# One kernel, its operand tiles moved: pairs of tiles at start addresses of their own

## The reference, cut to what matters

```
proj = rmsnorm(x) @ w_in                       # 1024 x 2048: pool channels, q, k, v
mk, mv = rmsnorm(mem) @ w_ck, rmsnorm(mem) @ w_cv
x = x + concat(pool_mix(u), moba_attend(q, k, v)) @ w_out
x = x + (softmax((rmsnorm(x) @ w_cq) mk^T / 16) mv) @ w_co
x = x + square(relu(rmsnorm(x) @ w_up)) @ w_down   # 1024 x 4096, 4096 x 1024
y = rmsnorm(x)
```

## Time and profile before

| | |
|---|---|
| median of 3 runs | 419.35 us |
| the profiled execution | 421.09 us |
| its span (first to last instruction) | 419.1 us |
| PE (matmuls) busy | 412.7 us, 98% |
| PEld (weight loads, beside the matmuls) | 386.7 us, 92% |
| VectorE (DVE) | 253.1 us, 60% |
| ScalarE (ACT) | 227.0 us, 54% |
| DMA | 96.60 MB, 230 GB/s |

### The profile page before, as it was taken

One profiled execution on the slowest core, in us unless ns is written; L12 is line 12 of the kernel. 1 busy time (PEld: TensorE's weight loads), 2 busy tenths in 40 slices (PEclk: granted clock), 3 DMA queues, 4 the chain that ended last, 5 costly groups with the idle time before them and its releaser, 6 DMA issues.

```text
span 419.1 us, 8425 instructions
## 1 busy us (share of the span) xinstructions
PE 412.7 (98%) x3372; PEld 386.7 (92%) x3372; DVE 253.1 (60%) x400; ACT 227.0 (54%) x392; POOL 30.9 (7%) x41
## 2 busy tenths in 40 slices
PE   9999999999999999999999999999999999999995
PEld 9998989986879998948899999999999999999995
DVE  4799989666355784633259777666667534454302
ACT  5876958725454664424267666566565433453313
POOL 1003026000000220000022000000000000010011
PEclk9999999999999999999999999999999999999999
DMA  8999858965988966989527646555565655545002
GB/s 288 384 386 359 283 194 251 349 253 191 404 295 317 386 218 226 370 309 335 218 102 248 205 141 199 185 187 163 184 200 196 196 172 192 183 158 185 2 2 103
DMA packets 37257, 96.60 MB, mean 230 GB/s; under 512 B 4186, under 2 KB 13274, under 8 KB 37082
## 3 DMA queue, kind: packets, MB, share of 16 engines
q1 hardware_dynamic: 35106, 92.24, 63.3%
q10 hardware_dynamic: 2112, 3.82, 2.5%
HBM read 91.73 MB, written 4.54 MB: 230 GB/s over the span
## 4 chain that ended last, share of the span: by engine, by line
PE 89%; DMA 5%; DVE 2%; SPq 1%; issue 1%; ACT 0%; DVEq 0%
PE psum L1104 75%; PE psum L826 4%; DMA raw<-in_w_in 2%; PE psum L1046 2%; PE psum L941 2%; DMA stage<-in_mem_v 2%; PE psum L954 1%; DMA pages<-in_page_table 1%; PE psum L838 1%; PE psum L878 1%; SPq L772 1%; PE psum L887 1%; PE psum L925 1%; PE psum L947 0%; DVE rstd L1586 0%
## 5 line engine op out<-in xcount | busy, mean ns | idle before, releaser
L1392 DVE TENSOR_TENSOR w_lo<-raw,w_hi 128x1024 fp32r<-128x1024 f32 x67 | 82.4, 1239 | 62.2 <-ACT w_hi L1124 62.0
L1124 ACT ACTIVATE w_hi<-raw 128x1024 fp32r<-128x1024 f32 (+1 forms) x73 | 74.0, 1021 | 60.7 <-PE psum L1104 45.4
L1104 PE MATMUL psum<-mix_hi,w_hi 128*128 128x264 f32 (+1 forms) x288 | 82.8, 287 | 0.0
L1104 PE MATMUL psum<-mix_lo,w_hi 128*128 128x264 f32 (+1 forms) x288 | 81.5, 283 | 0.0
L1104 PE MATMUL psum<-mix_hi,w_lo 128*128 128x264 f32 (+1 forms) x288 | 81.5, 283 | 0.0
L1104 PE MATMUL psum<-act_hi,w_hi 128*128 128x264 f32 x232 | 66.3, 286 | 0.0
L1104 PE MATMUL psum<-act_lo,w_hi 128*128 128x264 f32 x232 | 65.6, 283 | 0.0
L1104 PE MATMUL psum<-act_hi,w_lo 128*128 128x264 f32 x232 | 65.4, 282 | 0.0
L1104 PEld LDWEIGHTS psum<-mix_hi,w_hi 128*128 128x128 f32 x288 | 54.3, 188 | 0.9 <-issue 0.8
L1104 PEld LDWEIGHTS psum<-mix_lo,w_hi 128*128 128x128 f32 x288 | 54.3, 189 | 0.1
L1104 PEld LDWEIGHTS psum<-mix_hi,w_lo 128*128 128x128 f32 x288 | 54.3, 189 | 0.0
(11 more groups left out here) (208 smaller groups left out, 813.7 us busy)
## 6 DMA issues: line engine op xcount, KB each, us to landing
raw<-in_w_down SPq DMA_DIRECT2D x20, 512.0 KB, 3.3
raw<-in_w_up SPq DMA_DIRECT2D x18, 512.0 KB, 4.3
raw_more<-in_w_up SPq DMA_DIRECT2D x14, 512.0 KB, 3.7
stage<-in_mem_v SPq DMA_DIRECT2D x12, 512.0 KB, 6.5
raw_more<-in_w_down SPq DMA_DIRECT2D x12, 512.0 KB, 4.2
stage<-in_cache_v SPq DMA_DIRECT2D x16, 256.0 KB, 6.2
keysT<-in_cache_k SPq DMA_DIRECT2D x16, 256.0 KB, 5.0
keysT<-in_mem_k SPq DMA_DIRECT2D x8, 512.0 KB, 6.5
```

Of the source, the lines that this page charges most:

```text
L1104: mm = pe.matmul(out, a, b, start=first and m == 0, stop=end_ and m == 2)
L1124: return nc.scalar.activation(out, in_, ACT.Copy, scale=scale)
L1392: V.tensor_tensor(lo_of(c), raw_of(c), hi_of(c).bitcast(F32), ALU.subtract).then_inc(w_lo_ready, 1)
```

## The change

The parts of mix and hid are no longer one array with a fixed step. A function lays each tile at a residue of its own, from a list; the next free place with that residue is taken. Two tiles that follow each other (those of one chunk) share a residue. The high and the low part of a pair can have different ones.

```diff
+LINE = 64
+W_AT = 32
+MIX_HI, MIX_LO = [224, 224, 192, 0], [192, 32, 224, 32]
+HID_HI, HID_LO = [0, 32, 64, 96, 128, 160, 192, 224, 224, 224, 224, 224, 224, 240, 208, 16], [0, 32, 64, 96, 128, 160, 192, 224, 0, 32, 64, 128, 160, 240, 208, 16]
+MIX_AT = [r for part in (MIX_HI, MIX_LO) for r in part for _ in range(2)]
+HID_AT = [r for part in (HID_HI, HID_LO) for r in part for _ in range(2)]
...
-        sb("before_mix", [P, 40])
-        mix_hi = sb("mix_hi", [P, KT, PITCH], F32R)[:, :, 0:T]
-        mix_lo = sb("mix_lo", [P, KT, PITCH], F32R)[:, :, 0:T]
+        def tiles(name, columns, residues):
+
+            at, place = columns, []
+            for r in residues:
+                at += (W_AT + r // 4 - at) % LINE
+                place.append(at - columns)
+                at += T
+            whole = sb(name, [P, place[-1] + T], F32R)
+            return [whole[:, x:x + T] for x in place]
+
+        mix = tiles("mix", W_AT, MIX_AT)
+        mix_hi, mix_lo = mix[:KT], mix[KT:]
...
-        sb("before_act", [P, 48])
+        sb("before_act", [P, 8])
         act_hi = sb("act_hi", [P, KT, PITCH], F32R, early)[:, :, 0:T]
+        sb("between_parts", [P, 32], F32, early)
         act_lo = sb("act_lo", [P, KT, PITCH], F32R, early)[:, :, 0:T]
...
-        sb("beside_operands", [P, 1664])
+        sb("beside_operands", [P, 1696])
         raw_more = sb("raw_more", [P, MORE_RAW, CK, CN])
-        sb("before_more", [P, 8])
+        sb("before_more", [P, 40])
         w_hi_more = sb("w_hi_more", [P, MORE_SPLIT, CK, CN], F32R)
         w_lo_more = sb("w_lo_more", [P, MORE_SPLIT, CK, CN], F32R)
-        sb("before_hid", [P, 16])
-        hid_hi = sb("hid_hi", [P, FT, PITCH], F32R)[:, :, 0:T]
-        hid_lo = sb("hid_lo", [P, FT, PITCH], F32R)[:, :, 0:T]
+        hid_tiles = tiles("hid_tiles", 32, HID_AT)
+        hid_hi, hid_lo = hid_tiles[:FT], hid_tiles[FT:]
...
-                            passes = ((wh, mov_hi[:, k + kk, 0:N]), (wh, mov_lo[:, k + kk, 0:N]), (wl, mov_hi[:, k + kk, 0:N]))
+                            passes = ((wh, mov_hi[k + kk][:, 0:N]), (wh, mov_lo[k + kk][:, 0:N]), (wl, mov_hi[k + kk][:, 0:N]))
```

More of the change, by code:

```diff
@@ L1043, in last_by_tile @@
                             wh, wl = hi[:, kk, x * P:(x + 1) * P], lo[:, kk, x * P:(x + 1) * P]
-                            passes = ((wh, hid_hi[:, k + kk, :]), (wh, hid_lo[:, k + kk, :]), (wl, hid_hi[:, k + kk, :]))
+                            passes = ((wh, hid_hi[k + kk]), (wh, hid_lo[k + kk]), (wl, hid_hi[k + kk]))
                             for m, (a, b) in enumerate(passes):
@@ L1082, in _ @@
                 if w in ("in", "out", "co"):
-                    mov_hi, mov_lo = act_hi, act_lo
+                    mov_hi, mov_lo = ([t[:, i, :] for i in range(KT)] for t in (act_hi, act_lo))
                 elif w == "down":
@@ L1095, in _ @@
                             out = psum[:, bank, :]
-                            th, tl = mov_hi[:, k + kk, x * P:(x + 1) * P], mov_lo[:, k + kk, x * P:(x + 1) * P]
+                            th, tl = mov_hi[k + kk][:, x * P:(x + 1) * P], mov_lo[k + kk][:, x * P:(x + 1) * P]
                             passes = ((th, hi[:, kk, :]), (tl, hi[:, kk, :]), (th, lo[:, kk, :]))
@@ L1181, in take_out @@
                         wait_gemm_out(act, g, x)
-                        copy(mix_hi[:, k, :], xT[:, k, :], gains[:, GAIN[w], k:k + 1]).then_inc(stream_hi, 1)
+                        copy(mix_hi[k], xT[:, k, :], gains[:, GAIN[w], k:k + 1]).then_inc(stream_hi, 1)
                         square("c" if w == "out" else "f", k, xT[:, k, :], T)
@@ L1190, in take_out @@
                         act.wait_ge(square_ready, j + 1)
-                        copy(hid_hi[:, j, :], hid[:, 1, j % 2, :]).then_inc(hid_hi_ready, 1)
+                        copy(hid_hi[j], hid[:, 1, j % 2, :]).then_inc(hid_hi_ready, 1)
                     elif w == "down":
@@ L1239, in run @@
                     square("m", k, src, MEM)
-                    copy(mix_hi[:, k, 0:MEM], src, gains[:, GAIN["m"], k:k + 1]).then_inc(stream_hi, 1)
+                    copy(mix_hi[k][:, 0:MEM], src, gains[:, GAIN["m"], k:k + 1]).then_inc(stream_hi, 1)
                     return
@@ L1399, in low_of_square @@
                 dve.wait_ge(hid_hi_ready, j + 1)
-                V.tensor_tensor(hid_lo[:, j, :], hid[:, 1, j % 2, :], hid_hi[:, j, :].bitcast(F32), ALU.subtract).then_inc(hid_lo_ready, 1)
+                V.tensor_tensor(hid_lo[j], hid[:, 1, j % 2, :], hid_hi[j].bitcast(F32), ALU.subtract).then_inc(hid_lo_ready, 1)
             def make_qblock(src, table, first, rows):
@@ L1439, in take_out @@
                             dve.wait_ge(stream_hi, STREAM[w] + low + 1)
-                            less(mix_lo[:, low, :], xT[:, low, :], gains[:, GAIN[w], low:low + 1], mix_hi[:, low, :]).then_inc(stream_lo, 1)
+                            less(mix_lo[low], xT[:, low, :], gains[:, GAIN[w], low:low + 1], mix_hi[low]).then_inc(stream_lo, 1)
                     elif w == "cq":
@@ L1543, in run @@
                     dve.wait_ge(stream_hi, STREAM["m"] + k + 1)
-                    less(mix_lo[:, k, 0:MEM], memory(k), gains[:, GAIN["m"], k:k + 1], mix_hi[:, k, 0:MEM]).then_inc(stream_lo, 1)
+                    less(mix_lo[k][:, 0:MEM], memory(k), gains[:, GAIN["m"], k:k + 1], mix_hi[k][:, 0:MEM]).then_inc(stream_lo, 1)
                     return
```

## The result

The changed kernel took 421.19 us (median of 20 runs, 420.29 to 424.32), the kernel before 419.52 us (20 runs, 418.83 to 420.73). The ratio is 1.0038, 95% interval 1.0026 to 1.0050: 1.1 to 2.1 us slower, where 1.4 us faster was forecast, in a range from 416.8 to 420.8 us.

What follows compares the result with a forecast made beforehand. The prediction took the pace of PE's matmuls as the bound (TensorE busy 98%). Its terms, -1.24 - 0.28 + 0.28 - 0.12 = -1.36 us, took the 419.35 us median to 418.0 us; range 416.8 to 420.8 us.

Steps and rivals of the forecast that it cites:

- the three known points: Matmul paces before the change by residue to the weights: 224 gives 120.0 ns, 64 gives 120.97, 160 gives 121.66.
- the five terms: The forecast's changes in time by stage and tile, summing to -1.36 us.
- straight lines on the circle of 256 between the three known points: Weight matmuls at unmeasured residues: pace interpolated modulo 256 bytes, for example 0 at 120.32 ns, 128 at 121.43.
- the mean of its three passes, hi twice and lo once: Pace of a chunk with unlike high and low residues: averaged from its parts' paces, hi counted twice, lo once.
- Term 3: out, co and w_in's chunks, act_lo moved from 224 to 96: 0.40 ns a matmul, +0.28 us, ends 0 and +1.2.
- Term 1: cq and up, 960 matmuls on mix's four pairs: mean 120.37 ns against 121.66, -1.24 us, ends -3.2 and +1.6.
- Term 2: down, 768 matmuls on hid's sixteen pairs: 120.61 ns against 120.97, -0.28 us, ends -0.8 and +0.8.
- Terms 4 and 5: ck -0.12 us and cv 0 on mix's new places; the attention's moved tiles 0, ends +-0.2 us.
- Rival C: Weight matmuls of mix, act and down: unlike high and low residues break a rhythm; +2.5 us, 421.9 us; chance 0.19.
- turning point of 121.9 ns: Average cost of an unlike pair above which mix and act together lose what down wins, deciding the sign.
- The rule that spoke against the change: TensorE's weight load and moving operand have separate read ports, so no residue would matter and the time would stay.

Runs made afterwards that it cites:

- e5: Changed kernel with act and mix at residue 224, hid's sixteen pairs in down equal at 0, 16, ... 240; one run, 417.58 us.
- e6: Changed kernel with act and mix at 224, hid's high parts all at 0, low parts at 0, 16, ... 240; one run, 418.73 us.
- e1: Changed kernel with act_lo put back from residue 96 to 224, mix and hid keeping their new pairs; 419.81 us, ratio to the kernel before 0.9996.
- e2: Changed kernel with mix back at 160 and hid at 64, so only act_lo at 96 differs from before; 421.06 us, ratio 1.0031.
- e4: As e3, but mix_lo alone at residue 96; 419.37 us, ratio to the kernel before 0.9984.
- e8: Changed kernel with mix at (128, 128), hid at (0, 0) and act at (192, 224); one run, 421.65 us (before 418.92).
- e3: Changed kernel with act, mix and hid all at residue 224, high and low alike; 417.76 us, ratio to the kernel before 0.9951.
- e11: Changed kernel with act at (96, 224), hid at (32, 0) and mix at (96, 96); one run, 425.85 us (before 420.29).
- e9: As e3, with 64 bytes put ahead of everything, weights included, so only absolute addresses move; one run, 417.57 us.

## Why the prediction was wrong

**What held.** PE's pace is the bound; nothing else of the change cost time (ACT, DVE and PE's waits as forecast); the residue to the weights is a cause, and the three known points, 224, 64 and 160, repeated themselves in the chunks of down (120.2, 120.9, 121.8 ns).

**The step that failed is the one before the five terms: "straight lines on the circle of 256 between the three known points", and for a chunk "the mean of its three passes, hi twice and lo once".** Both halves are wrong, as e5 and e6 show. The sum missed by 3.0 us: 1.2 in act, 0.9 in cq and up, 0.7 in down, 0.2 in ck and cv. Its terms:

- Term 3, act: forecast +0.40 ns, +0.28 us. Measured +2.2 ns, +1.50 us (in 0.68, out 0.43, co 0.39). That is as much as the whole measured loss, though with this term alone put right the sum would still have said -0.1 us. Its upper end, +1.2 us, does not follow from its own numbers either: 123.3 ns over the 384 and half of the 312 matmuls is 1.8 us, and the 1.50 lies within that. e1 takes the loss away, e2 makes it alone, e4 gives it to mix: the pair (224, 96) has 122.2 ns, with equal pairs of its parts at 120.0 and 121.5.
- Term 1, cq and up: forecast -1.29 ns, -1.24 us. Measured -0.34 us. (224, 192) was to have 120.28 and has 122.0, (224, 32) 120.21 and 121.5; (192, 224), forecast at 120.55, is at 120.6, which is luck: its chunks settled to 120.0 and lost the rest on the way in, and e8 held it at 120.8. (0, 32), forecast at 120.43, could have 120.0 and had 121.5 because its chunk ended before the stream had settled.
- Term 2, down: forecast -0.28 us, measured +0.43. The five pairs with 224 high were the dear ones, 121.5 to 122.4, and 128 had 123.5.
- Terms 4 and 5: ck and cv together +0.06 us for -0.12. ck was slower by 1.0 ns, not faster: the points of 264 columns do not hold for its 256, as e3 shows. The attention's plain f32 matmuls kept their lengths (3.65 and 1.73 us in both chains).

**Rival C**, that unlike parts break a rhythm, was the nearest, and its price for act (1.6 ns for each matmul) was in the right place and too small. That its total of 421.9 us lies near is in part luck: its largest term was +1.6 us in mix, which measured -0.34. It made every unlike pair dear, but (0, 32), held long enough, has the best pace there is. Its turning point of 121.9 ns is also worked out wrongly: 960 matmuls of mix and 384 of act at one pace lose the 0.28 us that down was to win at 121.4 ns.

**The rule that spoke against the change.** The distances in e3, e5 and e11 are 120.0, 123.5 and 126.7 ns for the same instruction with no wait, and e9 shows that relative places count. The Trainium skill (SBUF — State Buffer, "Who interferes with whom") has PE with two independent read ports and says that PE waits on no one. If nothing held PE's reads up, no residue would matter, and here it does, by up to 6.7 ns; the measurement decides. That the two reads of PE hold each other up is the nearest reading and not shown: what ACT and DVE touch moved along in e9. Only the residue's effect is shown, not its mechanism.

**Open.** Which rhythm a stream takes: it depends on how it came in, but no rule was found that says it ahead. The changed kernel also scattered more (up to 424.32 us) than before (up to 420.73, and 422.37 in the 32 runs beside e1 to e4); nothing here was made to explain that.

## What to carry to other kernels

In this kernel, where weight loads and moving tiles stream without a gap, the pace of a matmul depends on the distance of their addresses modulo 256 bytes, by up to 6%; measure it as a count over a stretch, never by the duration of a record. Give all tiles of a stream one residue that holds its best pace from every start that occurs (here high and low at 224: 120.0 ns with 264 columns in all six stages that have them, 417.76 us), measure it for each width of the moving tile, and don't interpolate between measured residues or add up parts: a combination is a point of its own, and one visit of 24 matmuls may show only one of its rhythms. A sweep inside one kernel, a chunk for each candidate, is cheap, but the winner has to be held for a whole stage before it is believed.

## What the runs showed of the hardware

- With 264 columns whole stages were held at 120.0, 120.8, 121.0, 121.3, 121.5, 121.7, 122.2 and 123.3 ns, and 29 of up's 32 chunks at 126.7. None was held below 120.0, 10 ns over one column a cycle at the 2.4 GHz level.
- One combination can have two steps (128 with 128: 123.3, and 120.0 in single chunks only; 0 with 32: 120.0 and 121.2; 96 with 96: 121.8 and 126.7), and a single job of some matmuls between two chunks can put the stream from one to the other for the next 80 us.
- High and low exchanged can be the same, (224, 96) and (96, 224) 122.2, or not: (0, 32) 120.0, (32, 0) 122.2.
- The width of the moving tile changes the order of the places: with 256 columns (ck) the pair at 224 had 118.2 ns, that at 160 117.5, (224, 96) 117.4; with 264 columns 120.0, 121.7 and 122.2.
